# A mixture-of-experts stage whose gathered tokens are laid out by quarter, with six more weight pieces loaded into the quarters that are still empty

## What is computed

```
def expert_choice_ffn(h, w_router, w_gate, w_up, w_down):
    B, N, _ = h.shape
    cap = CAPACITY * N // N_EXPERTS
    aff = jax.nn.softmax((h @ w_router).astype(f32), -1)
    gate, idx = lax.top_k(jnp.swapaxes(aff, 1, 2), cap)
    bidx = jnp.arange(B)[:, None, None]
    xg = h[bidx, idx]
    g = jnp.einsum('becd,edf->becf', xg, w_gate)
    u = jnp.einsum('becd,edf->becf', xg, w_up)
    y = jnp.einsum('becf,efd->becd', jax.nn.silu(g) * u, w_down) * gate[..., None].astype(h.dtype)
    return jnp.zeros_like(h).at[bidx, idx].add(y)
```

## Time and profile before

| | us |
|---|---|
| median of 3 runs | 2391.23 (2391.07 to 2391.9) |
| the profiled execution's own time | 2391.57 |
| its span, first to last instruction | 2389.7 |
| PE busy | 2251.6 (94%) |
| experts' stage, first step of pair 0 to last down step | 515.9 to 780 |

### The profile page before, as it was taken

One profiled execution on the slowest core, in us unless ns is written; L12 is line 12 of the kernel. 1 busy time (PEld: TensorE's weight loads), 2 busy tenths in 40 slices (PEclk: granted clock), 3 DMA queues, 4 the chain that ended last, 5 costly groups with the idle time before them and its releaser, 6 DMA issues.

```text
span 2389.7 us, 28697 instructions
## 1 busy us (share of the span) xinstructions
PE 2251.6 (94%) x11081; PEld 1709.2 (72%) x11081; DVE 1234.8 (52%) x2315; ACT 852.1 (36%) x1498; POOL 363.9 (15%) x273
## 2 busy tenths in 40 slices
PE   7898988779879999999999999999999999999999
PEld 4685677655424676777888888886767788888887
DVE  4643455642102686667654434448776755543442
ACT  4433442432100445544342313334464334322231
POOL 0110123000000454432000000025533200000000
PEclk9999999999999999999999999999999999999999
DMA  8115410258999322221223333232222212333322
GB/s 297 56 46 197 139 36 11 97 186 321 363 387 337 100 71 71 62 79 54 80 89 98 97 97 97 90 92 71 81 61 71 71 58 84 106 99 97 97 87 80
DMA packets 198285, 281.48 MB, mean 118 GB/s; under 512 B 13278, under 2 KB 125448, under 8 KB 198152
## 3 DMA queue, kind: packets, MB, share of 16 engines
q1 hardware_dynamic: 197584, 278.47, 35.0%
q10 hardware_dynamic: 568, 1.19, 0.1%
HBM read 277.52 MB, written 2.10 MB: 117 GB/s over the span
## 4 chain that ended last, share of the span: by engine, by line
PE 76%; DVE 12%; DMA 5%; ACT 4%; issue 2%; SPq 1%; POOL 0%; DVEq 0%; ACTq 0%
PE PS L643 20%; PE PS L645 19%; PE PS L644 19%; PE PS L1401 3%; PE PS L2360 3%; PE PS L2400 2%; PE PS L1383 2%; DMA RX<-in_w_up_dram 1%; PE PS L2267 1%; DVE AL L846 1%; DMA RAW<-in_w_up_dram 1%; PE PS L1393 1%; PE PS L2416 1%; DVE AL L825 1%; DVE AL L838 1%
## 5 line engine op out<-in xcount | busy, mean ns | idle before, releaser
L643 PE MATMUL PS<-OPH,WHI 128*128 128x512 f32 x1224 | 498.3, 407 | 8.2 <-DVE OPL L1440 3.1
L645 PE MATMUL PS<-OPH,WLO 128*128 128x512 f32 x1224 | 481.5, 393 | 0.0
L644 PE MATMUL PS<-OPL,WHI 128*128 128x512 f32 x1224 | 480.5, 393 | 0.0
L594 ACT ACTIVATE WHI<-RAW 128x1024 fp32r<-128x1024 f32 (+2 forms) x286 | 295.5, 1037 | 470.7 <-PE PS L645 461.8
L631 POOL TENSOR_TENSOR WLO<-RAW,WHI 128x1024 fp32r<-128x1024 f32 (+1 forms) x107 | 255.8, 2394 | 1326.8 <-ACT WHI L594 1323.4
L615 DVE TENSOR_TENSOR WLO<-RAW,WHI 128x1024 fp32r<-128x1024 f32 x179 | 214.4, 1200 | 378.4 <-ACT WHI L594 378.4
L643 PEld LDWEIGHTS PS<-OPH,WHI 128*128 128x128 f32 x1224 | 231.9, 189 | 74.5 <-issue 22.5
L645 PEld LDWEIGHTS PS<-OPH,WLO 128*128 128x128 f32 x1224 | 231.8, 189 | 50.0
L644 PEld LDWEIGHTS PS<-OPL,WHI 128*128 128x128 f32 x1224 | 232.3, 190 | 43.6 <-issue 1.0
L643 PE MATMUL PS<-WHI,OPH 128*128 128x512 f32 (+2 forms) x576 | 231.4, 402 | 8.9 <-ACT AL L780 3.8
L645 PE MATMUL PS<-WHI,OPL 128*128 128x512 f32 (+2 forms) x576 | 218.0, 378 | 0.0
(11 more groups left out here) (431 smaller groups left out, 3283.6 us busy)
## 6 DMA issues: line engine op xcount, KB each, us to landing
RAW<-in_w_in_dram SPq DMA_DIRECT2D x102, 512.0 KB, 3.6
RAW<-in_w_ffn_in_dram SPq DMA_DIRECT2D x88, 512.0 KB, 3.5
RX<-in_w_gate_dram SPq DMA_DIRECT2D x42, 512.0 KB, 7.2
RX<-in_w_down_dram SPq DMA_DIRECT2D x42, 512.0 KB, 11.4
RAW<-in_w_ffn_out_dram SPq DMA_DIRECT2D x40, 512.0 KB, 3.4
RAW<-in_w_mod_dram SPq DMA_DIRECT2D x36, 512.0 KB, 4.5
RX<-in_w_up_dram SPq DMA_DIRECT2D x32, 512.0 KB, 10.0
RAW<-in_w_up_dram SPq DMA_DIRECT2D x25, 512.0 KB, 9.2
```

The lines of the kernel that those rows point to most:

```text
L594: hi.up(A.e.activation(q.fhi, q.flat, ACT.Copy), ("w", q.i))
L643: T.e.matmul(o, a[0], b[0], start=first, stop=False)
L644: T.e.matmul(o, a[0], b[1], start=False, stop=False)
L645: return T.e.matmul(o, a[1], b[0], start=False, stop=last)
```

## The change

The gathered tokens get the layout `p (x k n)`: the quarter first, so that each quarter is one closed range of 2048 elements of `FM`. The last two quarters, `FM[:, 4096:8192]`, give four places of 1024 elements. The experts' pieces 45 to 48 (the last three gate pieces and the first up piece of pair 2) go to these four places, and 67 and 68 (gate, pair 3) to the last two of them once more. These six no longer take a turn in the ring, so all later pieces sit in other slots. SP waits for `prod["slot"]` before a place's first use.

```
+    XGQ = FM[:, 0:8192].rearrange("p (x k n) -> p x k n", x=4, k=8)
...
+    QUARTERS = {45 + j: j for j in range(4)}
+    QUARTERS.update({67 + j: 2 + j for j in range(2)})
+    made, places_x, places_q = [0], {}, {}
 
     def expert_piece(w):
-        x = EXTRA.get(made[0])
+        x, y = EXTRA.get(made[0]), QUARTERS.get(made[0])
         made[0] += 1
+        if y is not None:
+            i = plan(w, 2, 512, False, True, at=FM[:, 4096 + 1024 * y:5120 + 1024 * y], place=places_q.get(y))[0]
+            if y not in places_q:
+                seq[i].after = "slots"
+            places_q[y] = seq[i].slot
+            return i
...
-        XG = in_(FM, 0, 8192).rearrange("p (k s) -> p k s", k=8)
+        XG = XGQ
...
-                o = XG[:, k, 256 * x:256 * x + 256]
+                o = XG[:, x, k, :]
...
-                moe_v.up(V.e.scalar_tensor_tensor(XG[:, k, 256 * x:256 * x + 256], ps(PB["xg", k, x], 256), BY["x2"](k),
+                moe_v.up(V.e.scalar_tensor_tensor(XG[:, x, k, :], ps(PB["xg", k, x], 256), BY["x2"](k),
...
-                            s0 = 64 * (2 * g + i)
-                            mm = T.e.matmul(PS[64 * i:64 * i + 64, 512 * b:512 * b + 512], XG[:, 2 * n + k, s0:s0 + 64],
+                            s0 = 64 * (2 * g + i) % 256
+                            mm = T.e.matmul(PS[64 * i:64 * i + 64, 512 * b:512 * b + 512], XG[:, g // 2, 2 * n + k, s0:s0 + 64],
...
+                elif q.after == "slots":
+                    Y.wait_ge(*prod["slot"])
```

More of the change, by code:

```diff
@@ L321, in body @@
     EXTRA.update({2 * (NRAW + NRX) + 8 + j: i for j, i in enumerate((2, 3, 6, 7))})
-    made, places_x = [0], {}
+    QUARTERS = {45 + j: j for j in range(4)}
+    QUARTERS.update({67 + j: 2 + j for j in range(2)})
+    made, places_x, places_q = [0], {}, {}
     def expert_piece(w):
-        x = EXTRA.get(made[0])
+        x, y = EXTRA.get(made[0]), QUARTERS.get(made[0])
         made[0] += 1
+        if y is not None:
[4 more added lines that the diff above has]
+            return i
         if x is None:
```

## The result

The changed kernel takes 2386.21 us (median of 17 runs, 2382.23 to 2391.22) where the kernel before, in the same session, takes 2389.88 (17 runs, 2386.37 to 2391.9): 3.67 us less, a ratio of 0.9985, 95% interval 0.9978 to 0.9991. The profiled execution took 2382.79 us, its span is 2381.1. Forecast were 3.6 us less. That it came out so near is luck in good part: two terms of the sum were off by 1.3 and by 0.8 us, and they have opposite signs; and the interval alone reaches from 2.2 to 5.3 us less. The forecast time, 2387.6 us, was counted from a median of 2391.23 over 3 runs of the kernel before; its median over 17 runs is 1.35 us lower, which is nearly all of the distance from 2387.6 to 2386.21.

A forecast was written before the change was run, and what follows sets the result against it. The prediction took weight transfers to bind the experts' stage, with DMA resting while the ring was full. Its terms, -4.8 + 1.2 = -3.6 us, gave a median of 2387.6 us, range 2385.8 to 2391.0.

The forecast's parts named there:

- The bound: Experts' stage: bound by weight transfers, DMA busy all the time from 634 to 750 us at 384 GB/s.
- Pair 2: Experts' pair 2: pieces 45 to 48 fill DMA's rest, so all three of PE's waits go, -2.06 us.
- Pieces 67 and 68: Experts' pair 3: with both pieces early in FM, its last step begins 4.8 us earlier, pair 2's term counted in.
- the free end: Rival: the stage gives all and ACT's delay at the end is made up, 2386.4 or 2385.8 us; chance 0.20.
- 5.4 if all eight waits vanish: Pairs 2 and 3: upper bound on the gain, 2.06 + 3.36 us, more than which PE alone can't give.
- Behind pair 3: Pair 4 to the stage's end: the whole stage moves by 4.8 us, and PE's waits stay.
- The turned ring: Stage's end: the third idx piece waits for the last down step, ACT's conversion begins later, +1.2 us; bounds 1.1 to 3.9.
- The clock: Rival at the stage's end: PE's clock falls for 8 us after a long wait, 2392.9 to 2394.3 us; chance 0.07.
- The clock is below 1.00 after it: Sign of a wrong prediction: granted clock below 1.00 after the first L703 at the stage's end.
- the late landing: Rival at the stage's end: the third idx piece lands after 6.0 us, 2390.3 us; chance 0.08.
- the moved rest: Rival: DMA stands still longer at the second rest, only pair 2's waits go, 2390.3 us; chance 0.10.
- The layout at nothing: Gathered tokens' new layout: same instructions and shapes, taken as 0 us; bounds 0 and some tenths.

The follow-up runs named there:

- e_all: The changed kernel plus thirteen more pieces in FM (49, 50, 69, 70, 91 to 94, 117 to 120, 141), to fill all rests: 2380.42 us, before 2390.63.
- c_changed: The changed kernel again, nothing altered, in another session as a control: 2389.08 us, kernel before 2391.80.
- e_late_six: Against the kernel before: new layout, six later pieces (117 to 120, 141, 142) in FM instead of the change's six: 2392.43 us, before 2391.80.
- e_turned: The changed kernel plus pieces 117 and 118 in FM, so the idx pieces come as early as before: 2386.67 us, kernel before 2391.80.
- e_third: The changed kernel plus four more pieces (91 to 94) in FM, for the third rest of DMA: 2381.69 us, kernel before 2390.63.
- e_layout: Against the kernel before: only the tokens' layout by quarter, no piece outside the ring: 2391.06 us, before 2391.00.
- e_turned_hi: As e_turned, with ACT making the three high halves of idx one by one behind squares: 2384.28 us, kernel before 2391.80.
- e_all_hi: As e_all, with ACT making the high parts of the index weights each behind a square: 2380.76 us, kernel before 2390.63.
- e_four: The changed kernel with only pieces 45 to 48 outside the ring, not 67 and 68: 2391.15 us, kernel before 2391.00.
- e_two: The changed kernel with only pieces 67 and 68 outside the ring, not 45 to 48: 2388.98 us, kernel before 2391.00.

## Why the prediction was right, and where its terms were off

- **The bound.** Right. The stage hangs on transfers, and a rest of DMA in it is worth about its own length. The three stretches of 5 us in which the changed kernel still rests, with shares of 0.78, 0.57 and 0.73 where a full one has 1.05, miss 5.1 us of transfer; filling them moved the stage's end by 5.1 us more, to 11.3. Where the share was full before (634 to 750), it and PE's busy time stayed as they were.
- **Pair 2.** The mechanism was right: three waits gone, none left. The term was mis-sized, -2.06 forecast and -2.72 measured. The step that failed is "all three waits go: -2.06", the sum of the idle times in brackets. An idle time is counted from the end of the last matmul, but matmuls that follow at once overlap, and a wait loses this overlap too. Eight matmuls with a wait ahead are shown at 1.94 us, and a step without a wait takes 1.72, so each wait costs 0.22 us more than its brackets say: 2.06 + 3 x 0.22 = 2.72. The prediction's 1.78 for a free step was a misreading as well: its 5.33 us run from the first start to the last end of three steps, so the last one counts with its tail.
- **Pieces 67 and 68.** Right in the mechanism, -4.8 forecast and -6.06 measured for the last step of pair 3. Of the 1.3 us, 0.7 is the term above: SP's issue behind pair 1's down step came 2.74 us sooner and not 2.06. The other 0.6 is the time from this issue to the last step: 604.35 - 585.58 = 18.77 us where 19.37 was worked out, with ten pieces in between, so a start-up of 5.1 us in place of 5.7. The prediction saw this (under the rival of the free end: 5.0 behind one rest, 5.7 behind the other) and took the larger. The bound "5.4 if all eight waits vanish, more than which PE alone can't give" was wrong, from idle times added up: seven waits went and gave 6.06, and in e_all, where pairs 2 and 3 have no wait left, the last step comes 7.14 us sooner. In c_changed, the same kernel, two waits are left and pair 3 gains 5.26, so half of the miss is no more than one run from the next.
- **Behind pair 3.** Right: -6.05 to -6.13 all through pairs 4 to 7, and -6.12 at the stage's end. The stage moved as one piece.
- **The turned ring.** Right in place, cause and nearly in size: a landing of 3.0 us in place of 3.2, a gap of 1.05 ahead of the third conversion, +0.92 us at L714 (+0.95 in c_changed, +1.17 in e_late_six) for a forecast of +1.2. e_turned, which takes the turn away, loses nothing there.
- **The clock.** What the sum took at nothing: the price of a fall. The forecast let PE stand still for 3.3 us and the clock at 1.00; PE stood still for 3.04, the clock fell to its lower level for some 3 us, and the chain lost 1.14 us (-5.20 to -4.06; c_changed 1.47). That this is the price of the fall rests on the comparison of traces: over the same part of the chain e_third and e_all, where the clock fell, lost 1.14 and 1.19, and before, e_layout, e_late_six and e_turned, where it did not, lost at most 0.02 us (e_turned_hi and e_all_hi, with another order on ACT and no fall, lost 0.4). "The clock is below 1.00 after it" was one of the prediction's own signs of being wrong, and it came. Its argument against a fall, that 2.12 us of idle time had left the clock alone, did not carry over to 3 us. The rival had a fall of 8 us, behind a wait of 6.0 us, at 2.6 to 4 us. So it came in part, with the forecast and not in its stead, at about half its lowest price. The gap of 6.17 us ahead of 498.99 that it was taken from ended with DVE and not with a transfer.
- **The sum.** -6.1 + 0.9 + 1.1 = -4.1 at the end of the chain and -3.7 at the end of the run, against -4.8 + 1.2 = -3.6. The last 0.35 us are lost behind the end of the chain, and their cause is open. The errors of the stage (-1.3) and behind it (+0.8 to the end of the chain, +1.2 to the end of the run) nearly cancel: the mechanism of the stage and of the ring is right, the nearness of the sum is luck. Of the rivals, the free end is out (the end did take 2.1 us), the late landing too (3.0 us), and the moved rest is what happens with the four pieces alone. The layout at nothing: shown by e_layout. The wait for `prod["slot"]`, which e_layout does not have, cost nothing either: SP issues the `FM` pieces right behind the last `RAW` piece.

## What to carry to other kernels

Where a stage hangs on transfers and its profile still has stretches with the DMA at rest, the rest is the reserve: any memory that is idle just then, even for one turn, is a place to load into, and its worth here was about the rest's length, and more than the sum of the waits that PE shows. Cost a wait step to step (start of this step less start of the last, less what a step takes undisturbed), not by the idle time in brackets. And when the number of loads through a ring changes, follow the ring to its end: which slots does the next block's first load get, and who reads them last; two pieces more or less decided here over some 2.5 us of a gain of 5 to 6.

## What was not expected of the hardware

- The granted clock fell to its lower level behind the stage's end in some traces and not in others, for some 3 us each time, at a price of 1.1 to 1.5 us. The idle time of PE just ahead of it does not decide alone. It fell behind 3.04 (the change), 3.07 (c_changed), 4.17 (e_four) and 3.96 us (e_two), and did not behind 2.12 (before), 1.88 (e_turned, e_layout) and 1.56 us (e_turned_hi, e_all_hi); but it fell behind 1.88 us in e_third and e_all, and did not behind 3.29 us in e_late_six. All these are single profiles; what else it hangs on stays open, and was not tried.
- The core drew 386 GB/s for 116 us on end (629 to 745, share 1.05) in the changed kernel, 384 in e_third and e_all from 660 to 740. The Trainium skill, page "DMA: Bandwidth & Descriptors", section Specifications, has about 358 GB/s as the limit of a core, worked out there as a stack's bandwidth divided by two cores. This program runs on one core, and its traces are above that; what two cores at once would draw, no run here shows.
- With all rests filled PE still waits in pairs 4 to 7: the idle times there that name a transfer add up to 16.6 us in e_all, and to 19.6 in before and in the change. The stage is still bound by transfers. In the changed kernel the share is 0.01 and 0.00 over 500:505 and 505:510, just ahead of pair 0; whether pieces could be loaded there was not tried.
